# Expert layers with gathered rows against whole tables read block by block: one core, a three-layer token mixer

## The reference, cut to what matters

```python
def block(xb):                                     # xb: 256 tokens x 1024
    q = (xb @ w_q).reshape(T, 8, 2, 128)
    s = einsum('thcd,hcnd->thcn', q, sub_keys)     # 128 scores per head and half
    top_s, top_i = top_k(s, 16)
    cand = top_s[:, :, 0, :, None] + top_s[:, :, 1, None, :]
    best_s, best_c = top_k(cand.reshape(T, 8, 256), 16)
    i1, i2 = top_i[:, :, 0][best_c // 16], top_i[:, :, 1][best_c % 16]
    e = i1 * 128 + i2                              # 8 x 16 = 128 of 16384 experts per token
    gate = softmax(best_s)
    act = gelu(einsum('td,ted->te', xb, expert_u[e]))
    return einsum('te,ted->td', gate * act, expert_v[e])
```

## Time and profile before

| | us |
|---|---|
| median of 3 runs (lowest, highest) | 2536.98 (2535.01, 2539.37) |
| the profiled execution, its own time | 2530.09 |
| its span | 2528.3 |
| PE busy | 2247.8 (89%) |
| PE weight loads | 1265.8 (50%) |
| DVE busy | 1659.6 (66%) |
| ACT busy | 911.9 (36%) |
| POOL busy | 871.4 (34%) |
| DMA | 945.41 MB, mean 374 GB/s |

### The profile page before, as it was taken

How to read it: one execution, slowest core, us unless ns; L and a number is a source line. 1 busy time by engine, 2 the same in 40 slices (tenths; PEclk the granted TensorE clock), 3 DMA queues, 4 the chain that set the end, 5 groups by cost and what they waited for, 6 DMA issues and landing times.

```text
span 2528.3 us, 29579 instructions
## 1 busy us (share of the span) xinstructions
PE 2247.8 (89%) x9630; PEld 1265.8 (50%) x9630; DVE 1659.6 (66%) x3972; ACT 911.9 (36%) x2668; POOL 871.4 (34%) x796
## 2 busy tenths in 40 slices
PE   9998889998988989899999898989899989977776
PEld 7887644554444535544535554435555536522222
DVE  3864366666665677566776566767567766776664
ACT  2232133333343433243443334533244533423232
POOL 0012033334343343343443343334343344344442
PEclk9999999999999999999999999999999999999999
DMA  5420489999999999999999999999999999999996
GB/s 194 133 85 19 185 314 421 421 421 421 422 418 421 415 386 421 421 420 422 419 395 421 421 421 420 422 417 407 421 416 391 410 421 420 414 416 421 421 417 287
DMA packets 152443, 945.41 MB, mean 374 GB/s; under 512 B 16955, under 2 KB 19147, under 8 KB 53861
## 3 DMA queue, kind: packets, MB, share of 16 engines
q0 software_dynamic: 110592, 805.36, 77.0%
q1 hardware_dynamic: 41700, 138.20, 14.2%
HBM read 942.44 MB, written 1.05 MB: 373 GB/s over the span
## 4 chain that ended last, share of the span: by engine, by line
PE 45%; DMA 39%; DVE 7%; ACT 4%; issue 3%; POOL 1%; DVEq 0%; SPq 0%; ACTq 0%; POOLq 0%
DMA arena<-in_uv,idx 39%; PE bank L1875 26%; PE bank L354 7%; DVE arena L1903 4%; PE bank L1532 2%; PE bank L1520 2%; ACT arena L1941 1%; PE bank L825 1%; PE bank L585 1%; PE bank L841 1%; PE bank L1427 1%; ACT arena L1929 1%; PE bank L812 1%; PE bank L866 1%; ACT arena L1935 1%
## 5 line engine op out<-in xcount | busy, mean ns | idle before, releaser
L1875 PE MATMUL bank<-arena 128*128 128x512 f32 x3072 | 1449.6, 617 | 246.5 <-ACT arena L1941 240.7
L1960 POOL DMA_INDIRECT arena<-in_uv,idx x768 | 843.7, 1099 | 1435.6 <-PE bank L1875 1298.8
L1875 PEld LDWEIGHTS bank<-arena 128*128 128x128 f32 x3072 | 574.0, 195 | 968.8 <-issue 614.3
L1903 DVE CUSTOM_DVE_ANT_0 arena<-arena,h 128x1024 f32<-128x1024 f32 x512 | 627.3, 1225 | 415.7 <-DMA arena<-in_uv,idx 400.9
L1929 ACT ACTIVATE arena<-arena 128x2 f32<-128x2 f32 x384 | 78.2, 204 | 1226.7 <-DVE arena L1903 1226.5
L1903 DVE CUSTOM_DVE_ANT_0 arena<-arena 128x1024 f32<-128x1024 f32 x256 | 313.7, 1225 | 218.0 <-DMA arena<-in_uv,idx 210.7
L354 PEld LDWEIGHTS bank<-xT,weights 128*128 128x128 f32 x2032 | 279.8, 191 | 57.5 <-issue 39.6
L354 PE MATMUL bank<-xT,weights 128*128 128x128 f32 (+2 forms) x2032 | 299.6, 303 | 0.0
L1941 ACT ACTIVATE arena<-const,arena 128x128 f32<-128x128 f32 x768 | 260.5, 386 | 0.0
L1935 ACT ACTIVATE arena<-arena 128x1 f32<-128x1 f32 x768 | 184.8, 288 | 12.6
L1929 ACT ACT_TABLE_LOAD x73 | 93.7, 1283 | 1.3
(11 more groups left out here) (331 smaller groups left out, 1766.4 us busy)
## 6 DMA issues: line engine op xcount, KB each, us to landing
weights<-in_w_q SPq DMA_DIRECT2D x50, 512.0 KB
weights<-in_w_in SPq DMA_DIRECT2D x38, 512.0 KB
weights<-in_a_fm SPq DMA_DIRECT2D x28, 512.0 KB
arena<-in_uv,idx POOLq DMA_INDIRECT x768
weights<-in_a_out SPq DMA_DIRECT2D x16, 512.0 KB
weights<-in_b_fm SPq DMA_DIRECT2D x16, 512.0 KB
weights<-in_b_out SPq DMA_DIRECT2D x16, 512.0 KB
arena<-in_w_q SPq DMA_DIRECT2D x14, 512.0 KB, 13.1
```

What stands on the lines that cost most here:

```text
L1875: ins = nc.tensor.matmul(acc[:, :], diag[:, e % DIAGS, :], ring[:, e % RING, at:at + 512], start=first, stop=last)
L1903: V.tensor_tensor_reduce(out=u, in0=u, in1=x, scale=1.0, scalar=0.0, op0=ALU.mult, op1=ALU.add, accum_out=dots[:, unit % 2, kx:kx + 1]).th ...
L1960: nc.gpsimd.indirect_dma_start(out=ring[:, s, :], out_offset=None, in_=io[f"uv{unit // PH // NT}"], in_offset=bass.IndirectOffsetOnAxis(ap ...
```

## The change

The gathers, the ring, the dot products on VectorE and the diagonals go. The tables are laid out anew: `ut` as 128 blocks [1024 in 8 pieces x 128 experts i1] for each i2, `vt` as 128 blocks [128 experts i1 x 1024] for each i2. They are read in full through the six slots, as any other weight, and each block serves all 256 tokens. `u_pair` multiplies two u blocks with all tokens into one bank, and ScalarE writes Gelu of it into `acts` (128 x 128 x 256, expert i1 on partitions). Meanwhile VectorE does top-k, with one softmax exponential on ScalarE in every third pair. Indices i1, i2 and gates are kept in `picks` and transposed (`picksT`), so that a token's 128 picks lie on partitions. Then, for each token, ScalarE makes a one-hot matrix of i1 (Relu(1 - (i1 - iota)^2)), VectorE one of i2 times the gate, and PE multiplies them: a 128x128 map of the token's gates over all experts. Four tokens make a turn (`TURNS` = 64 a layer); VectorE multiplies the four maps into `acts`. Then the v blocks are multiplied with `acts` into four banks.

The order by hand goes: each engine runs queries, u, gates, v, norm, mixer, norm, layer after layer, and the mixers take both token tiles at once (`two_*`, `three_*`, `tm_out`, `enter_tensor`). Memory keys and values move to the end of the first mixer. GpSimd has no work after the first mixer.

```diff
-                    nc.gpsimd.indirect_dma_start(
-                        out=ring[:, s, :], out_offset=None, in_=io[f"uv{unit // PH // NT}"],
-                        in_offset=bass.IndirectOffsetOnAxis(ap=idx[:, unit % 2, kx:kx + 1], axis=0)
-                    ).then_inc(sem(f"landed_uv_{s}"), 16)
...
+            for c in range(CHUNKS):
+                block_of(("ut", n, c), io[f"ut{n}"][c])
+            for c in range(CHUNKS):
+                block_of(("vt", n, c), io[f"vt{n}"][c])
...
+        def u_pair(pe, n, p):
+            job = ("u", n, p)
+            for half in range(2):
+                c = 2 * p + half
+                pe.wait_ge(*landed(("ut", n, c)))
...
+                for kc in range(KC):
+                    ins = nc.tensor.matmul(out[:, half * TOK:(half + 1) * TOK], w[:, kc * P:(kc + 1) * P], x_all[:, kc, :],
+                                           start=kc == 0, stop=kc == KC - 1)
...
+        def peer_tensor(pe, n):
...
+            for p in range(PAIRS):
+                u_pair(pe, n, p)
+                if p == PAIRS // 2:
+                    picks_tensor(pe, n, 0)
+            picks_tensor(pe, n, 1)
+            for turn in range(TURNS):
+                pe.wait_ge(*banks.take(("spread", n, turn)))
+                out = banks.bank(("spread", n, turn))
+                pe.wait_ge(sem("hot1_ready"), TURNS * n + turn + 1)
+                pe.wait_ge(sem("hot2_ready"), TURNS * n + turn + 1)
+                for x in range(TOGETHER):
+                    at = TOGETHER * (turn % 2) + x
+                    ins = nc.tensor.matmul(out[:, x * P:(x + 1) * P], hot1[:, at, :], hot2[:, at, :], start=True, stop=True)
+                ins.then_inc(banks.full_sem(("spread", n, turn)), 1)
...
+            for c in range(CHUNKS):
+                pe.wait_ge(*landed(("vt", n, c)))
+                w = slot(("vt", n, c))
+                for i in range(NT):
+                    for half, acc in enumerate(v_banks(n, i)):
+                        ins = nc.tensor.matmul(acc[:, :], acts[:, c, cols_of(i)], w[:, 512 * half:512 * half + 512],
+                                               start=c == 0, stop=c == CHUNKS - 1)
...
+            for p in range(PAIRS):
+                job = ("u", n, p)
+                act.wait_ge(*banks.full(job))
+                if 2 * p == FREE_CHUNKS:
+                    act.wait_ge(sem("gate_ready"), (n + 1) * UNITS)
+                nc.scalar.activation(acts[:, 2 * p:2 * p + 2, :],
+                                     banks.bank(job)[:, :].rearrange("p (a b) -> p a b", a=2),
+                                     ACT.Gelu).then_inc(banks.emptied_sem(job), 1)
+                if p % 3 == 2 and unit < UNITS:
+                    softmax_exp(act, n * UNITS + unit)
...
+            for turn in range(TURNS):
+                if turn > 1:
+                    act.wait_ge(*banks.full(("spread", n, turn - 2)))
+                at = TOGETHER * (turn % 2)
+                for x in range(TOGETHER):
+                    t = TOGETHER * turn + x
+                    ins = nc.scalar.activation(hot1[:, at + x, :], k("iota"), ACT.Square, scale=-1.0,
+                                               bias=picksT[:, 0, t:t + 1])
+                ins.then_inc(sem("apart"), 1)
+                act.wait_ge(sem("apart"), TURNS * n + turn + 1)
+                both = hot1[:, at:at + TOGETHER, :]
+                nc.scalar.activation(both, both, ACT.Relu, scale=-1.0, bias=ones[:, 0:1]).then_inc(sem("hot1_ready"), 1)
...
+            def hot_two(turn):
+                if turn > 1:
+                    v.wait_ge(*banks.full(("spread", n, turn - 2)))
+                for x in range(TOGETHER):
+                    t = TOGETHER * turn + x
+                    ins = V.tensor_scalar(hot2[:, t % HOTS, :], k("iota"), picksT[:, 1, t:t + 1], picksT[:, 2, t:t + 1],
+                                          ALU.is_equal, ALU.mult)
+                ins.then_inc(sem("hot2_ready"), 1)
+
+            hot_two(0)
+            for turn in range(TURNS):
+                if turn + 1 < TURNS:
+                    hot_two(turn + 1)
+                job = ("spread", n, turn)
+                v.wait_ge(*banks.full(job))
+                t = TOGETHER * turn
+                to = acts[:, :, t:t + TOGETHER]
+                out = banks.bank(job)[:, :].rearrange("p (t c) -> p c t", t=TOGETHER)
+                V.tensor_tensor(to, to, out, ALU.mult).then_inc(banks.emptied_sem(job), 1)
```

More of the change, by code:

```diff
@@ L270, in build, with plan_mem @@
             block_of(("rwkv_out", j), io["w_rwkv_out"][j])
[L272 to L281, removed]
+        def plan_mem(n):
             for j in range(2):
@@ L353, in fm_tile @@
             for kc in range(KC):
[L354 to L369, removed]
                 ins = nc.tensor.matmul(out[:, 0:n], w[:, kc * P:(kc + 1) * P], x[:, kc, :],
@@ L1631, in score_area @@
-        def score_area(w):
-            return 0 if w == 0 else 1
-        def first_slot(group, step):
-            return PH * group - 23 + step
-        def mem_slot(piece):
-            return MEM_SLOT + piece * 5 // 8
-        def scores_tensor(pe, job, queries, block, i, at, n):
-            w = slot(block)
-            pe.wait_ge(*banks.take(job))
-            out = banks.bank(job)
-            for x in range(n):
-                ins = nc.tensor.matmul(out[:, x * P:(x + 1) * P], queries[:, at + x, i], w[:, x * P:(x + 1) * P],
-                                       start=True, stop=True)
-            ins.then_inc(banks.full_sem(job), 1)
@@ L1770, in first_scalar @@
[L1770 to L1778 removed]
+            for i in range(NT):
+                fm_wait(pe, 0, i)
+        def first_scalar(act):
@@ new lines, in two_tensor @@
+            for i in range(NT):
+                for par in range(2):
+                    r = slice(64 * par, 64 * par + 64)
+                    pe.wait_ge(*banks.take(("attn", i, par)))
+                    out = banks.bank(("attn", i, par))
+                    for j in range(3):
+                        ins = nc.tensor.matmul(out[:, j * P:(j + 1) * P], kf[r, j, i * P:(i + 1) * P],
+                                               qf[r, j, i * P:(i + 1) * P], start=True, stop=True)
+                    ins.then_inc(banks.full_sem(("attn", i, par)), 1)
@@ new lines, in two_tensor @@
+            pe.wait_ge(sem("o_squares"), 1)
+            for x_ in range(3):
+                pe.wait_ge(*banks.take(("os", x_)))
+                out = banks.bank(("os", x_))
+                nc.tensor.matmul(out[:, :], ones, rs[:, 2 * x_:2 * x_ + 2, :].rearrange("p a b -> p (a b)"),
+                                 start=True, stop=True).then_inc(banks.full_sem(("os", x_)), 1)
+            ready = {6: [banks.emptied(("mo", 0, i)) for i in range(NT)]}
+            ready.update({2 * x_: [(sem("o_gated"), x_ + 1)] for x_ in range(3)})
```

1816 lines of the change are left out of this document (699 added, 1117 removed).

## The result

The changed kernel takes 3950.89 us, the median of four runs (3947.34 to 3952.28), where the kernel before took 2535.99 beside it: ratio 1.558, 95% interval 1.555 to 1.562. Its profiled execution took 3952.23 us for a span of 3950.6. The forecast was 3980, 0.7% above.

A forecast was written before the change was run, and what follows sets the result against it. It took gather transfers to bound the kernel before, with PE near its limit. Front 353, experts 3252, mixers 170 and 182 and end 18 sum to 3975 us of span; 5 added give 3980, range 3930 to 4060.

The forecast's parts named there:

- Front: Work before the experts, with memory keys and values and other pieces moved before the queries: experts start at 353 us.
- Table stages: u and v products over whole tables, per layer: PE records times pitch, 442 and 440 us, table reads costing nothing.
- Turns: Gate spreading between u and v: ScalarE decides, 2.0 us a turn, 64 a layer; bounds 1.85 and 2.9.
- Mixers: Gated linear attention and stick-breaking, both token tiles at once, now on the path: 170 and 182 us.
- End: End of the kernel: 14 us for two norms and 4 for the output, 18 us.
- Sum: Whole kernel: front, three expert layers, two mixers and end, 3975 us of span, plus 5 to the median.
- A: Gate turns slower, by VectorE's strided product at half rate or hand-overs in series: 4120 us; chance 0.17.
- B: Table loads in the gate turns, Relu and Square in different sets, 493 us: 4470 us; chance 0.03.
- C: Long dense u and v products don't keep the full clock, getting 0.94: 4150 us; chance 0.05.
- D: Edges shorter than forecast, waits under other work, 60 to 80 us less: 3910 us; chance 0.09.
- F: The change doesn't replace the gathers, or computes only the chosen blocks; nothing given as its chance.
- E: Whole kernel faster than before because bytes decide; table products at a quarter of the price give 1990 us; chance 0.02.

The follow-up runs named there:

- thin blocks: Changed kernel reading only the first 128 of 1024 columns of each of the 768 table blocks: 3950.34 us, ratio 1.557.
- halved u: Changed kernel with u products summing only 4 of the 8 pieces of 128 features, blocks still read whole: 3289.03 us.
- cut v: Changed kernel with the v products alone on the upper 16 bits of each float32, bytes read unchanged: 3118.81 us.
- cut kernels: Changed kernel with u and v products on the upper 16 bits of each float32: 2354.12 us; with exponentials also moved ahead: 2283.15 us.
- Both runs on the kernel before: Kernel before, expert sums' products on the upper 16 bits of each float32: 2527.88 us; kernel before, gathering u rows only: 2258.82 us.
- cut sums: Kernel before with the expert sums' products on the upper 16 bits of each float32, all else as it was: 2527.88 us, ratio 0.9975.

## Why the prediction was right

**Front.** 353 forecast, 353.7 measured.

**Table stages.** 2048 x 0.216 and 1024 x 0.429 gave 442 and 440; measured 442.4 and 441.4 in the first layer and within 2 us of it in the others. v's start at the low clock, which the forecast had, is in it: at the first v the clock was 0.51 over 990.5 to 994, and the third v, at 1.00 throughout, took 439.7. The pitch of the records was the step on which everything hung. The thin blocks, the halved u and the cut v show that it alone sets these stages. That the table reads cost nothing holds: 3950.89 and 3950.34 with and without seven eighths of them.

**Top-k under u.** The forecast was 167 us of VectorE under the 442, and up to 167 more without that cover; 158 a layer came with the cover taken away.

**Turns.** 2.0 forecast, 1.92 measured, ScalarE as the bound. The sum of ScalarE's parts, 1.27 + 0.72 less overlap = 1.95, was right to 0.03; I rounded up for gaps, and there were none. VectorE's product, which steps by 512 bytes in the bank from element to element and by 1 KB in `acts` after every fourth, took 0.687, as the plain one: nothing stood behind the upper bound of 2.9. Relu between Squares had no table load. The Trainium skill (ScalarE: Activation LUTs, section Table sets) says that relu is in every set, and the trace agrees: no load in 192 turns.

**Queries and a layer.** 67 forecast, 67 and 69 measured. A layer from first query to last sum is 1078.1, 1080.1 and 1077.9 against 1084; the 6 us are those of the turns.

**Mixers.** 170 and 182 forecast, 165.7 and 180.2 measured, but by two errors that cancel. In the first I had 130 us of products and 40 of bare waits and norms; measured are 159.2 us of PE busy and 6.5 idle. PE's waits by line, in the two windows of the mixers of the changed kernel (line <- what it waited for: us, times, longest), the longest of each:

```profile
PE bank L2026 <- ACT arena L2087: 2.2, 1, 2.2
```
```profile
PE bank L2241 <- DVE arena L2309: 8.9, 2, 7.9
```

The reciprocals that I took for 10 us of bare wait in the first mixer were hidden. Three reciprocals of 3.35 us each ran from 1552 to 1564, while PE worked on. In exchange PE was busy where I had idle time: 24 records of L1430, the norms' rows, take 16.0 us (8 of them in front, 16 behind the mixer), and the transpositions (L1493) 6.7. The granted clock was 0.88, which I had priced at 1.00; 0.12 x 159 is 19 us, an estimate of what that cost over rows, transpositions and products together. In the second the idle 19 us come near the 20 of waits, and PE's 161 takes the place of 137 + 14 + 11. The terms were mis-sized by up to 30 us, and the sum by 2 to 4: that the sum was right here was luck.

**End.** 18 forecast, 14.9 measured.

**Sum.** 3975 for the span against 3950.6: 16 from the layers, 4 and 2 from the mixers, 3 from the end, less 1 at the front make 24 of the 24.4. The 5 us added for the distance of a profiled execution to the median weren't there.

**Rivals.** A fell: the turns were not slower but faster. B fell: no table load in them. C fell in the plateaus (clock 1.00), but the clock was low in the mixers, where it costs some 20 us each, an estimate, and was part of no term. D, edges shorter by 60 to 80, had the right sign and a third of the size. F fell with the queue table. E, the bytes decide, was wrong for the change as it is. The cut kernels made its condition true: there a product costs PE about a quarter, and the kernel is faster than before. Its price was mis-sized, though. I had 3975 - 0.75 x 2650 = 1990, by which a stage takes 110 us; with PE that fast the transfers' 165 us decide, 3975 - 2650 + 6 x 165 = 2315, and 2283 was measured. The rival left out its own mechanism.

**The bound of before.** The prediction read from shares of 1.00 and 89% that transfers decide and PE is near. Both runs on the kernel before bear it out: less PE work gives 0.25%, fewer bytes 11%.

## What to carry to other kernels

Before reading a table whole in place of gathering from it, hold the products of the whole table in the kernel's own type against the time of the gathered bytes: here each table stage costs 442 us of float32 products where its transfers need 165, so bytes were saved where they no longer counted. The same change is a gain of 7% over the float32 kernel before once a product costs about a quarter, and of 10% with the exponentials moved as well; a change of layout and a change of type have to be priced together, and on both sides. And a cover is only as long as what lies over it: top-k cost nothing under 442 us of u, and was the limit under 165, until its exponentials were asked for earlier.

## What was not expected of the hardware

- **Stepped operands of TensorE.** A bfloat16 view that takes the upper half of each float, so every second 16 bits, ran at nearly four times the pace of float32: four products of 512 columns took 1.08 us, the last record being 0.39, so 0.23 each, against two records at 0.429 for each float32 product. A bfloat16 operand without steps is in no run. The weight load took 98 ns instead of 190. The Trainium skill (VectorE: DVE Perf Modes, section on the TRN2 errata) has 216 ns for a product of 512 columns; the runs come near it in bfloat16, and float32 costs four times as much, 0.86.
- **The clock under half load.** In the turns PE was busy 29.4 of 50 us (900 to 950), in gaps of 0.79 us behind each eight records, and kept 1.00. In the kernel before with cut sums it was busy 1267 of 2167 us, nearly the same share, with gaps of 0.55 to 3.20 us in front of its sums (1000 to 1020), and had 0.72. Part of that busy time is the lower clock itself: a record of the sums took 523 ns in the mean, against 391 for the same shape in the cut v. What sets the two apart, the length of the gaps or the work in them, was not tried.
- **Equal work can get a different clock.** The same mixer had 0.88 in the changed kernel and 0.90 in the kernel without Relu, and took 165.7 or 161.2 us. Executions of one kernel differ less: 0.980 to 0.983 in four of the changed one. Of the 83 us between those two spans 21 lie in such stretches, so a difference of two spans isn't all the price of an edit.
